# Attention heads in pairs on TensorE, three exponential buffers, and the running sums over keys in two products

## The reference

```python
for l in range(2):
    x = x + 0.5 * rms_norm(swiglu_ffn(rms_norm(x, ...), ...), ...)
    x = x + rms_norm(hybrid_mixer(rms_norm(x, ...), w_in[l], ...), ...)
    x = x + 0.5 * rms_norm(swiglu_ffn(rms_norm(x, ...), ...), ...)
```

```python
z = jnp.einsum('bhqd,bhkd->bhqk', q_blk, k) * scale
earlier = key_pos[None, :] < query_pos[:, None]
log_keep = jnp.where(earlier, jax.nn.log_sigmoid(-z), 0.0)
log_stick = lax.cumsum(log_keep, axis=3, reverse=True) - log_keep
w = jnp.where(earlier, jnp.exp(jax.nn.log_sigmoid(z) + log_stick), 0.0)
return jnp.einsum('bhqk,bhkd->bhqd', w, v)
```

## Time and profile before

| | us |
|---|---|
| median of 3 runs | 2056.57 (2054.72 to 2056.75) |
| the profiled execution's own time | 2056.11 |
| its span, from the first to the last instruction | 2054.2 |
| TensorE busy | 2019.0 (98%) |
| VectorE busy | 1321.5 (64%) |
| ScalarE busy | 1103.4 (54%) |

### The profile page before, as it was taken

The page is one execution under the profiler, slowest core; times in us unless marked ns, Lnnn a source line. Parts: engine busy times, 40 slices in busy tenths (PEclk is TensorE's granted clock), DMA queues, the critical chain, the costliest instruction groups (busy, mean ns, idle before and its releaser), DMA issues.

```text
span 2054.2 us, 27823 instructions
## 1 busy us (share of the span) xinstructions
PE 2019.0 (98%) x11020; PEld 1701.4 (83%) x11020; DVE 1321.5 (64%) x2158; ACT 1103.4 (54%) x1722; POOL 74.1 (4%) x149
## 2 busy tenths in 40 slices
PE   7999999999989999999999999999999999999998
PEld 4988899987767788888898788888888898788887
DVE  4456566655775656655597886655755587887653
ACT  4345455445454445654646666544654646666552
POOL 0000000001010000000100000000000100000000
PEclk9999999999999999999999999999999999999999
DMA  9786576665355746756534366554755534357551
GB/s 343 253 294 223 175 264 199 202 222 180 103 185 186 260 169 195 225 174 215 186 119 138 124 223 218 184 184 154 229 191 189 203 123 151 118 186 250 182 180 51
DMA packets 281905, 392.92 MB, mean 191 GB/s; under 512 B 9596, under 2 KB 175916, under 8 KB 281648
## 3 DMA queue, kind: packets, MB, share of 16 engines
q1 hardware_dynamic: 277616, 379.62, 56.3%
q0 software_dynamic: 3184, 9.04, 1.3%
q10 hardware_dynamic: 976, 2.49, 0.3%
HBM read 390.06 MB, written 1.05 MB: 190 GB/s over the span
## 4 chain that ended last, share of the span: by engine, by line
PE 86%; DMA 4%; issue 3%; DVE 3%; ACT 2%; POOL 1%; SPq 0%; DVEq 0%; POOLq 0%; ACTq 0%
PE bank L875 21%; PE bank L911 21%; PE bank L913 21%; PE bank L912 21%; DMA raw<-in_ffn_w_in 2%; DVE wlo L2078 1%; PE bank L1036 1%; DMA raw<-in_w_mod 1%; ACT whi L1478 1%; PE bank L959 1%; DVE tm L2884 0%; ACT junk L1538 0%; DMA mlm<-in_mlm 0%; DMA pm<-in_pool 0%; ACT full L1549 0%
## 5 line engine op out<-in xcount | busy, mean ns | idle before, releaser
L2078 DVE TENSOR_TENSOR wlo<-raw,whi 128x1024 fp32r<-128x1024 f32 x360 | 433.9, 1223 | 316.6 <-ACT whi L1478 314.7
L1478 ACT ACTIVATE whi<-raw 128x1024 fp32r<-128x1024 f32 x360 | 375.0, 1057 | 404.9 <-PE bank L913 210.9
L911 PE MATMUL bank<-whi,xTh 128*128 128x512 f32 (+1 forms) x1344 | 527.4, 392 | 5.6 <-issue 3.6
L913 PE MATMUL bank<-whi,xTl 128*128 128x512 f32 (+1 forms) x1344 | 520.6, 387 | 0.0
L912 PE MATMUL bank<-wlo,xTh 128*128 128x512 f32 (+1 forms) x1344 | 520.1, 387 | 0.0
L2083 DVE SCALAR_TENSOR_TENSOR wlo<-raw,cols,whi 128x512 fp32r<-128x512 f32 (+2 forms) x608 | 407.0, 721 | 155.5 <-ACT whi L1483 152.1
L1483 ACT ACTIVATE whi<-raw,cols 128x512 fp32r<-128x512 f32 (+2 forms) x608 | 385.4, 696 | 147.1 <-PE bank L913 110.5
L911 PEld LDWEIGHTS bank<-whi,xTh 128*128 128x128 f32 x1344 | 252.6, 188 | 60.0 <-issue 8.4
L913 PEld LDWEIGHTS bank<-whi,xTl 128*128 128x128 f32 x1344 | 252.4, 188 | 52.2
L912 PEld LDWEIGHTS bank<-wlo,xTh 128*128 128x128 f32 x1344 | 252.7, 188 | 48.6
L875 PE MATMUL bank<-xTh,whi 128*128 128x256 f32 x696 | 198.0, 285 | 0.3 <-DVE wlo L2078 0.3
(11 more groups left out here) (368 smaller groups left out, 2454.7 us busy)
## 6 DMA issues: line engine op xcount, KB each, us to landing
raw<-in_w_in SPq DMA_DIRECT2D x68, 1024.0 KB, 5.2
raw<-in_ffn_w_in SPq DMA_DIRECT2D x132, 512.0 KB, 6.1
raw<-in_ffn_w_gate SPq DMA_DIRECT2D x88, 512.0 KB, 4.1
raw<-in_ffn_w_up SPq DMA_DIRECT2D x88, 512.0 KB, 5.1
raw<-in_ffn_w_down SPq DMA_DIRECT2D x40, 1024.0 KB, 5.0
raw<-in_w_mod SPq DMA_DIRECT2D x36, 1024.0 KB, 6.3
raw<-in_ffn_w_out SPq DMA_DIRECT2D x30, 1024.0 KB, 5.2
raw<-in_w_out SPq DMA_DIRECT2D x12, 1024.0 KB, 5.0
```

The costliest lines, as they stand in the source:

```text
L911: e.matmul(o, hi[:, kc, sl], wh[:, c], start=at == 0 and k == 0, stop=False)
L913: ins = e.matmul(o, lo[:, kc, sl], wh[:, c], start=False, stop=fin)
L1478: e.activation(wh, raw, ACT.Copy).then_inc(m.whi_done, 1)
L2078: e.tensor_tensor(wl, raw, wh.bitcast(F32), ALU.subtract).then_inc(m.wlo_done, 1)
```

## The change

Three edits in the mixers of the last two layers:

- `scores` and `values` on TensorE take two heads at a time, p = 0 to 3. The products of the two heads alternate: keys block 0 of head 2p, of head 2p+1, then keys block 1 of each. scores(p) stands in steps 0, 2, 4 and 6, values(p) in steps 3, 5, 7 and 9. `value_mm` now counts pairs.
- `ex` has three buffers instead of two (h % 3), and ScalarE's wait ahead of Abs changes with it.
- `sticks` has two products instead of three: NL meets all 384 columns of spl at once, NO the last 128.

The exponentials on ScalarE, the step on VectorE and their order are as before, a head at a time.

```diff
-        self.ex, o = self.at(o, "ex", [128, 2, 384])
+        self.ex, o = self.at(o, "ex", [128, 3, 384])
...
+        def values(p):
+            b, _ = self.t.bank["bo", l, p // 2]
+            bank, cs = m.psum[b], p % 2 * 256
+            for h in (2 * p, 2 * p + 1):
+                self.evacuated("sc", l, h)
+            if p % 2 == 0:
+                self.bank("bo", l, p // 2)
+                if p == 0:
                     self.evacuated("sv", l, 1)
...
+            for i, n in ((0, 256), (1, 128)):
+                for h in (2 * p, 2 * p + 1):
+                    pr, hc = slice(h % 2 * 64, h % 2 * 64 + 64), slice(h * 64, h * 64 + 64)
+                    ins = self.mm(bank[pr, cs + 256 - n:cs + 256], m.sv[:, i, hc], m.ex[:, h % 3, i * 256:i * 256 + n],
+                                  i == 0 and p % 2 == 0, i == 1 and p % 2 == 1)
+            ins.then_inc(m.full[b] if p % 2 else m.value_mm, 1)
...
-            self.mm(bank[:, 0:256], NL, m.spl[:, r, 0:256], False, False)
-            self.mm(bank[:, 128:256], NO, m.spl[:, r, 256:384], False, False)
-            self.mm(bank[:, 256:384], NL, m.spl[:, r, 256:384], False, True).then_inc(m.stick_mm, 1)
...
+            self.mm(bank[:, 0:384], NL, m.spl[:, r, :], False, False)
+            self.mm(bank[:, 128:256], NO, m.spl[:, r, 256:384], False, True).then_inc(m.stick_mm, 1)
+
+        def scores(p):
+            if p == 0:
                 self.evacuated("sk", l, 1)
                 e.wait_ge(m.mask_done, l + 1)
...
+            pair = [self.bank("sc", l, h) for h in (2 * p, 2 * p + 1)]
+            for i, n in ((0, 256), (1, 128)):
+                for x, (bank, _) in enumerate(pair):
+                    pr = slice(64 * x, 64 * x + 64)
+                    self.mm(bank[:, i * 256:i * 256 + n], m.kT[pr, p, i * 128:i * 128 + 128], m.qT[pr, p, 256 - n:256], i == 0, False)
+            for bank, full in pair:
+                o = bank[:, :].rearrange("p (a n) -> p a n", a=2)[:, :, 0:128]
+                self.mm(o, m.one2[:, :], m.maskr[:, :, :], False, False).then_inc(full, 1)
...
-            if 2 <= n < 10:
-                values(n - 2)
+            if n in (3, 5, 7, 9):
+                values((n - 3) // 2)
             if 1 <= n < 9:
                 sticks(n - 1)
-            if n < 8:
-                scores(n)
+            if n in (0, 2, 4, 6):
+                scores(n // 2)
...
-            x = m.ex[:, h % 2, :]
-            if h == 5:
+            x = m.ex[:, h % 3, :]
+            if h in (5, 6):
                 self.filled("bo", l, 0)
-            elif h >= 2:
-                e.wait_ge(m.value_mm, 6 * l + h - 1 - (h - 2 >= 4))
+            elif h >= 3:
+                e.wait_ge(m.value_mm, 2 * l + 1 + (h == 7))
```

More of the change, by code:

```diff
@@ L1287, in mixer @@
         step = [0]
[L1289 to L1295, removed]
-                    self.evacuated("sv", l, 1)
[L1297 to L1301, removed]
+        def values(p):
[6 more added lines that the diff above has]
+                if p == 0:
+                    self.evacuated("sv", l, 1)
+            for i, n in ((0, 256), (1, 128)):
[4 more added lines that the diff above has]
+            ins.then_inc(m.full[b] if p % 2 else m.value_mm, 1)
         def sticks(h):
@@ L1942, in sticks @@
             b, n = self.t.bank["sc", l, h]
-            e.activation(m.ex[:, h % 2, :], m.psum[b][:, 0:384], ACT.Exp).then_inc(m.free[b], 1)
+            e.activation(m.ex[:, h % 3, :], m.psum[b][:, 0:384], ACT.Exp).then_inc(m.free[b], 1)
         def scores(h):
             bank, _ = self.filled("sc", l, h)
-            x = m.ex[:, h % 2, :]
-            if h == 5:
+            x = m.ex[:, h % 3, :]
+            if h in (5, 6):
                 self.filled("bo", l, 0)
-            elif h >= 2:
-                e.wait_ge(m.value_mm, 6 * l + h - 1 - (h - 2 >= 4))
+            elif h >= 3:
+                e.wait_ge(m.value_mm, 2 * l + 1 + (h == 7))
             e.activation(x, bank[:, 0:384], ACT.Abs).then_inc(m.act, 1)
@@ L2777, in scores @@
                 e.wait_ge(m.stick_mm, 8 * l + h - 1)
-            e.scalar_tensor_tensor(out=m.spl[:, h % 2, :], in0=bank[:, 0:384], scalar=0.0, in1=m.ex[:, h % 2, :],
+            e.scalar_tensor_tensor(out=m.spl[:, h % 2, :], in0=bank[:, 0:384], scalar=0.0, in1=m.ex[:, h % 3, :],
                                    op0=ALU.max, op1=ALU.add).then_inc(m.spl_done, 1)
```

## The result

| | before | after |
|---|---|---|
| median, us | 2055.64 (4 runs, 2053.13 to 2056.75) | 2044.92 (4 runs, 2043.87 to 2047.52) |
| own time and span of the profiled execution | 2056.11, 2054.2 | 2043.87, 2042.0 |

The ratio is 0.9952, its 95% interval 0.994 to 0.9964: faster by 10.7 us, between 7.4 and 12.3. The forecast was 9.0 us and 2047.6.

The account below looks back on a forecast made before the run. The prediction took TensorE as the bound, VectorE close behind at 88%. Per layer, 8.2 us of work removed less 3.7 of waits gave 4.5, twice 9.0, so 2047.6 us for the median, range 2044.0 to 2051.5.

Parts of the forecast that it names:

- What bounds it: Both layers' attention stage: TensorE busy all 55 us and alone on the path, VectorE close behind at 88%.
- The work removed: TensorE per layer: paired scores save 3.4 us plus 0.8 at masks, paired values 3.2 plus 0.8 before sticks; 8.2 together.
- the toll at a change of shape: TensorE in an attention step: 0.14 us ahead of values, 0.20 ahead of others, whenever the array's use changes shape.
- again 0.2: The mask on TensorE: its single pass takes 0.107 us and the remainder, charged to a shape change, is 0.2.
- The waits: TensorE waiting for VectorE's spl: 1.86 us at sticks(1), 1.15 at sticks(5), 0.65 at sticks(7); 3.7 per layer.
- The walk of VectorE: Step-by-step timing of VectorE through layer 0's attention, with a two-tap step of 4.96 us, giving each spl's time.
- Behind the stage: After the attention: VectorE 3.7 us earlier, TensorE 4.5, the 2.3 us lead at heads() shrinks by 0.8; gain goes through.
- A: TensorE pairs don't overlap: 0.5 us gained per layer, 2055.6 us, chance 0.05; one kind only, 2050.4 to 2051.4, chance 0.07.
- B: TensorE passes start strictly in order: a pair costs 0.86 us instead of 0.65, 3.6 gained per layer, 2049.4; chance 0.07.
- C: Turning between heads' array halves costs a drain, no overlap: a pair costs 1.7 us, slower at 2062.0; chance 0.03.
- D: VectorE less tight, the waits at sticks(5) and sticks(7) don't come: 6.3 us gained per layer, 2044.0; chance 0.04.
- E: VectorE slower, its eight taps 0.6 us longer a step: 1.7 us gained per layer, 2053.2; chance 0.02.

Follow-up runs that it names:

- e1: The kernel before with the convolution's taps in the attention steps left out (14 of 31 per layer less one); 2071.30 us, stage 55.16 us.
- e9: The kernel before with four taps per layer moved out of attention steps 1 to 4, ahead of the attention; 2053.17 us, stage 55.16 us.
- e2: The changed kernel with the convolution's taps in the attention steps left out; 2056.43 us, stage 48.06 us.
- x2: The changed kernel with four taps moved ahead of the attention and, in odd steps, ScalarE's scores(n) ahead of sticks(n-1); 2040.36 us, stage 47.89 us.
- e3: The changed kernel with values one head at a time again, so scores alone in pairs; 2048.20 us, stage 51.91 us.
- e4: The changed kernel with scores one head at a time again, so values alone in pairs; 2048.76 us, stage 51.96 us.
- x3: x2 with spl ahead of the tap in odd steps and two chunk states moved from step 7 to 8 on VectorE; 2044.99 us, stage 48.75 us.
- e5: The changed kernel with both heads of a scores pair on array rows 0 to 63; 2048.07 us, stage 52.46 us.
- e6: The changed kernel with all of one head's products issued before the other's, in scores and values; 2046.93 us, stage 50.54 us.
- e8: The changed kernel with two exponential buffers instead of three; 2072.24 us, stage 64.76 and 61.73 us in the two layers.

## Why the prediction was right

The result, 2044.92, is 2.7 us under the forecast and inside the range. By its steps:

**What bounds it.** Right. TensorE alone set the stage's end before (e1 and e9: less or other work on VectorE, 55.16 as ever), and VectorE has a share in it after (e2).

**The work removed**, forecast 8.2 us a layer. The gaps over 0.23 sum to 1.69+0.92+0.51 = 3.1 us; each of these sticks also holds up the next product by 0.1 more (1.06 for 0.96, 0.89 for 0.78), its weight load lying bare. So the waits cost 3.4, and 4.65+3.4 = 8.05 was removed. From x2, whose waits are 0.11, 0.52 and twice 0.1, it is 55.16-47.89+0.83 = 8.1. By kind, e3 gives 3.25+0.81 = 4.1 (forecast 3.4+0.8 = 4.2), e4 3.2+0.70+0.10 = 4.0 (3.2+0.8). Overlap is full in both, and the toll at a change of shape is saved as forecast. Single records of before, in step 1, divide this toll of 0.20: the last pass of scores starts at 1100.81 and takes 0.108, the mask starts at 1101.01 and the next product at 1101.23. So 0.09 lies ahead of the new product's start and 0.11 behind it, where its weight load lies bare. So between the mask's start and the next product, 0.22 us in the earlier trace rows, only 0.11 is toll; the "again 0.2" of the prediction includes the 0.09 ahead of the mask, and the sum of a step isn't touched.

**The waits**, forecast 1.86, 1.15 and 0.65, in all 3.7. They are 1.8, 1.0 and 0.6, at these three and nowhere else. The walk of VectorE holds to 0.1 us: with 2.96 added for the later start of before, spl 1, 4, 5 and 7 are at 1104.06, 1121.80, 1127.36 and 1137.49, where it had 1104.04, 1121.8 to 1121.9, 1127.4 and 1137.4. The waits were 0.25 us too large in sum and the work 0.1 too large; so 4.65 us a layer for 4.5. Of the terms ahead of a late sticks, the semaphore took 0.05 (0.06 forecast; spl(1) ends at 1101.65 and sticks(1) starts at 1101.70), and the 0.11 for the weights lies inside sticks(1), not ahead of it, which is the 0.1 counted above.

**Behind the stage.** VectorE has z ready at 1154.74, on the clock of before 1157.70, 3.9 us earlier than the earlier trace rows (forecast 3.7). heads() starts at 1156.32, so the lead shrank from 2.3 to 1.6 us and held. x3 shows what it costs when it is spent.

**The rivals.** A, no overlap, is refuted by e3 and e4, and e5 shows for the scores what it would cost; B by e6; C by the pairs' 0.92 and 0.87 us; D by the waits themselves; E by spl's times. The slower side came about in e8 alone, by a part of the change that I had costed at nothing on the condition that it is there.

**The difference of the medians**, 10.7 us, is 1.4 over the 9.3 of the stages. Its interval holds both. The likeliest reason is the start of the mixer, which differs by up to 3.5 us between the executions profiled here; with four runs a side this isn't averaged out, and no run tests it. So of the 2.7 us by which the forecast time was missed only 0.3 is the change (9.3 for 9.0); 0.9 is the median before, 2055.64 in four runs where the forecast started from 2056.57, and 1.4 is this rest, which the forecast did not explain.

## What to carry to other kernels

When TensorE is busy all the time and another engine at nearly 90%, work taken from TensorE is worth its price only up to the point where the other engine's next result is late; walk that engine through the stage instruction by instruction, and afterwards look for what it can do elsewhere (here four taps a layer, worth 2.4 us a layer after the change and nothing before it). A wait on an in-order engine is filled by what stands ahead of it, so a reorder that brings one result forward must be followed through to the next one (x3). And for changes of a few us compare stages between fixed products, which repeat to 0.05 us, rather than totals, which move by 3 to 4.

## What I had not expected of the hardware

- The order of issue within a pair hardly matters: stage 50.54 head by head, 50.51 in turn (e6). Passes for two halves of the array pair up even when two passes of one half are issued first.
- A weight load is hidden under the products ahead of it, but not behind a wait, nor behind a change of shape. In after, from the start of sticks to the next product it is 0.78 us at sticks(0), which has neither, 0.89 at sticks(7) with a wait, and 0.89 at sticks(4) and (6), which wait for nothing and stand behind values.
- After 5.5 us without a product in e1 the granted clock was 0.50 for the next 4.6 us, that is 1.2 GHz, and mu took 3.22 us from its start to the next product, 1.53 before. In e8 no idle stretch of TensorE in the stage is longer than 2.41 us, and yet the clock fell: TensorE was busy 3.05 and 2.54 of 4 us in two windows, the clock had a mean of 0.63 in the second and 0.51 in the third, though TensorE was busy for all of that. A wait of 2.35 us from 1110.6, by itself, had left it at 1.00. In after, with waits of at most 1.5 us in its products, it stayed at 1.00.
